# One program for the output stage and the experts of a hybrid decoder step, with the routing tables built inside the first expert block

## What is computed

```python
xp = xp + mod_p[:, 2] * yp                       # output stage
h  = modulate(x, g_ffn, shift, scale)            # RMS norm, scale and shift
top_logit, top_idx = lax.top_k(h @ w_router + b_router, 4)   # 4 of 32 experts
top_w = softmax(top_logit)
# for every expert e, in blocks of 128 of its rows:
gate = min(xb @ w_gate[e] + b_gate[e], 7)
up   = clip(xb @ w_up[e] + b_up[e], -7, 7)
f[rows] += top_w * (((up + 1) * gate * sigmoid(1.702 * gate)) @ w_down[e] + b_down[e])
y = rmsnorm(x + mod[:, 5] * f, g_final)
```

## Time and profile before

| | us |
|---|---|
| median of three timed runs | 1798.55 |
| profiled execution, its own time | 1795.53 |
| span of the profiled execution, first to last instruction | 1793.5 |
| TensorE busy in the span | 1688.0 (94%) |
| VectorE busy | 1425.5 (79%) |
| ScalarE busy | 1099.8 (61%) |

### The profile page before, as it was taken

One profiled execution on the slowest core, in us unless ns is written; L12 is line 12 of the kernel. 1 busy time (PEld: TensorE's weight loads), 2 busy tenths in 40 slices (PEclk: granted clock), 3 DMA queues, 4 the chain that ended last, 5 costly groups with the idle time before them and its releaser, 6 DMA issues.

```text
span 1793.5 us, 27031 instructions
## 1 busy us (share of the span) xinstructions
PE 1688.0 (94%) x9028; PEld 1312.8 (73%) x9028; DVE 1425.5 (79%) x1361; ACT 1099.8 (61%) x1045; POOL 333.4 (19%) x309
## 2 busy tenths in 40 slices
PE   4999978888998799999999999999999999999996
PEld 2776767555554478888888888888888888888884
DVE  4422564476426789999999999999999999999997
ACT  4212343455333367777777777777777777777773
POOL 0000021300101012223222222322222232223211
PEclk9999989699999689999999999999999999999998
DMA  9454553620226579999999999999999999999993
GB/s 348 172 185 171 107 156 101 209 96 7 77 87 200 219 269 355 382 371 377 375 378 376 371 377 376 373 375 375 378 371 381 377 373 376 382 374 374 386 351 125
DMA packets 114598, 516.08 MB, mean 288 GB/s; under 512 B 25870, under 2 KB 47710, under 8 KB 62058
## 3 DMA queue, kind: packets, MB, share of 16 engines
q1 hardware_dynamic: 101082, 483.48, 71.5%
q0 software_dynamic: 12800, 29.45, 5.9%
q10 hardware_dynamic: 656, 2.36, 0.3%
HBM read 502.75 MB, written 31.09 MB: 298 GB/s over the span
## 4 chain that ended last, share of the span: by engine, by line
PE 62%; DVE 1%; DMA 1%; ACT 0%; issue 0%; SPq 0%; POOL 0%; DVEq 0%; POOLq 0%; ACTq 0%
PE banks L2965 58%; PE banks L2973 3%; PE banks L2951 1%; DMA routing<-in_g_final 0%; DMA ffn_rows<-weighed,block_rows 0%; DVE split L3167 0%; DVE arena L3264 0%; PE banks L3020 0%; ACT split L3079 0%; DVE arena L3257 0%; DVE arena L3256 0%; SPq L2885 0%; POOL wait_taken L2903 0%; DVEq L2831 0%; DVE gates L3180 0%
## 5 line engine op out<-in xcount | busy, mean ns | idle before, releaser
L2965 PE MATMUL banks<-split 128*128 128x512 f32 x4608 | 1076.0, 393 | 1.1 <-DVE split L3167 1.1
L2965 PEld LDWEIGHTS banks<-split 128*128 128x128 f32 x4608 | 860.4, 188 | 185.9 <-issue 7.2
L3167 DVE TENSOR_TENSOR split<-expert_buffers,split 128x2048 fp32r<-128x2048 f32 x384 | 864.8, 2284 | 41.7 <-ACT split L3079 39.5
L3079 ACT ACTIVATE split<-expert_buffers 128x2048 fp32r<-128x2048 f32 x384 | 733.2, 1918 | 216.6 <-PE banks L2965 212.2
L2903 POOL TENSOR_TENSOR wait_taken<-routing 128x1 f32<-128x1 f32 x62 | 76.4, 1232 | 811.8 <-PE banks L2973 464.5
L2926 POOL DMA_INDIRECT ffn_rows<-weighed,block_rows x31 | 107.7, 3473 | 4.8 <-issue 4.8
L662 PE MATMUL banks<-w_in_high,hT_high 128*128 128x476 f32 x192 | 75.8, 395 | 4.6 <-DVE hT_low L498 4.6
L3171 DVE TENSOR_TENSOR split<-banks,split 128x1024 fp32r<-128x1024 f32 x64 | 77.8, 1215 | 0.7 <-ACT split L3082 0.7
L662 PE MATMUL banks<-w_in_high,hT_low 128*128 128x476 f32 x192 | 73.3, 382 | 0.0
L3082 ACT ACTIVATE split<-banks 128x1024 fp32r<-128x1024 f32 x64 | 64.5, 1008 | 6.1 <-PE banks L2973 6.1
L573 DVE COPY arena<-banks 128x476 f32<-128x476 f32 x12 | 7.8, 654 | 70.0 <-PE banks L662 69.9
(11 more groups left out here) (396 smaller groups left out, 1733.2 us busy)
## 6 DMA issues: line engine op xcount, KB each, us to landing
expert_buffers<-in_w_gate SPq DMA_DIRECT2D x128, 1024.0 KB, 7.8
expert_buffers<-in_w_up SPq DMA_DIRECT2D x128, 1024.0 KB, 17.9
expert_buffers<-in_w_down SPq DMA_DIRECT2D x128, 1024.0 KB, 7.4
arena<-in_w_ada SPq DMA_DIRECT2D x16, 1024.0 KB, 4.9
w_in_landing<-in_w_in SPq DMA_DIRECT2D x5, 1904.0 KB, 8.9
arena<-in_w_ada SPq DMA_DIRECT2D x4, 2048.0 KB, 19.8
arena<-in_x_prompt SPq DMA_DIRECT2D x8, 512.0 KB, 9.4
arena<-in_cache_cmp SPq DMA_DIRECT2D x32, 128.0 KB, 2.9
```

What stands on the lines that cost most here:

```text
L2965: last = pe.matmul(ps[:, bank + c, :], x[:, kt * P:(kt + 1) * P].bitcast(F32R), wt.bitcast(F32R), start=(m == 2 and kt == 0 and x is xs[0] ...
L3079: act.activation(high[:, j % RING_Q].bitcast(F32R), v, ACT.Copy).then_inc(s_high, 1)
L3167: dve.tensor_tensor(rest[:, j % RING_Q].bitcast(F32R), v, high[:, j % RING_Q], ALU.subtract).then_inc(s_rest, 1)
```

## The change

The two stages become one, `output_and_experts`, with one set of engine programs. `router_programs` returns the router's programs, of which each expert program first runs its engine's, and some late pieces as functions that are called within the first expert block.

- The first block always is expert 0. Its rows are no longer gathered: `first_rows(t)` multiplies the rows h2 of tile t (as the stationary operand, float32) with 0/1 marks `in_first`, and gives the turned block directly. `take_rank` forms these marks with two more operations.
- `take_rank(t)` and `place(t)` stand one tile earlier; `choose(3)` stands behind the rows of the last tile, not before. Tiles 3 and 4 are placed together, behind rest 2 of the first block; their shares stand behind rest 1.
- The marks and the table's sums use the rounded format, with the weight as two parts (96 columns instead of 64); the 20 matmuls of the table (`tables`) stand inside the first gate, `turn_shares` behind it, and `begin_sums` between the quarters of the first up.
- ScalarE's four first `begin_read` stand between its high parts of the first block and of block 1's gate, the fifth in step 1.
- `count_blocks` and `place_overflow` stand at the start of VectorE's step 16 (COUNT_AT), the matmuls of the marks behind TensorE's 16th up in the rounded format with 3 x 18 columns instead of 2 x 17 in float32, the second `write_table` between `read_up` and `activate` of that step, and the 16th `down` waits for it. The registers are loaded behind step 16. Until then block k is expert k, and SP loads no register for it.
- SP starts the first three weight quarters after the last output projection, the other three after the last tile's rows; the bias of expert 0 is loaded after them.

The core of the diff (in the new text; lines that were only moved are left out):

```diff
-STAGES = [project, gla, compress, prompt_attention, sample_attention, output_and_router, experts]
+STAGES = [project, gla, compress, prompt_attention, sample_attention, output_and_experts]
+COUNT_AT = 16
+WIDE = OVER + 1
...
+        def first_rows(t):
+            n = TILES[t][1]
+            pe.wait_ge(s_in_first, t + 1)
+            v = h2[t].rearrange("s (p k) -> s k p", k=KT)
+            for kt in range(KT):
+                last = pe.matmul(ps[:, 6 + kt // 4, (kt % 4) * P:(kt % 4 + 1) * P], v[0:n, kt, :], in_first[t][0:n, :],
+                                 start=(t == 0 and kt % 4 == 0), stop=(t == ST and kt % 4 == 3))
...
+        for t in range(NT):
+            project_out(t, range(KT // 2))
+            if t >= 2:
+                ranks(t - 2)
+            project_out(t, range(KT // 2, KT))
...
+            if t >= 1:
+                turn_rows(t - 1)
                 if t >= 2:
+                    first_rows(t - 2)
+                route(t - 1)
+        turn_rows(ST)
+        ranks(ST - 1)
+        route(ST)
+        first_rows(ST - 1)
+        ranks(ST)
+        first_rows(ST)
+        ranks(NT)
...
+            one = first1[0:m, t:t + 1]
+            link(dve.scalar_tensor_tensor(one, ps[0:m, 3, t * NE:t * NE + 1], 1.0, selb[0:m, t, 0:1], ALU.add, ALU.mult))
+            dve.tensor_scalar(in_first[t][0:m, :], core.const("iota_p")[0:m, :], 1.0, one, ALU.add, ALU.is_equal
...
-            gate(0, 0)
-            up(0, 4)
-            turn_rows(1, first=True)
-            overflow()
+            def first_block():
+                pe.wait_ge(s_ones, 1)
+                pe.wait_ge(router.s_lg, NT)
+                pe.wait_ge(router.s_cnt, 1)
+                start_with_bias(0, 1, GB)
+                start_with_bias(1, 1, UB)
+                pe.wait_ge(s_xt, 1)
+                product(0, (xh, xl), GB, 0, range(2))
+                pe.wait_ge(s_xt, 2)
+                product(0, (xh, xl), GB, 0, range(2, 3))
+                tables()
+                product(0, (xh, xl), GB, 0, range(3, 4))
+                turn_shares(range(ST))
+                turn_shares(range(ST, NT))
+                product(1, (xh, xl), UB, 4, range(1))
+                begin_sums(0)
+                product(1, (xh, xl), UB, 4, range(1, 2))
+                begin_sums(1)
+                product(1, (xh, xl), UB, 4, range(2, 3))
+                begin_sums(2)
+                turn_rows(1, first=True)
+                product(1, (xh, xl), UB, 4, range(3, 4))
+                begin_sums(3)
...
+                up(k, first_of(prev) + 4)
+                if counted:
+                    pe.wait_ge(s_y, prev)
+                    overflow()
                 if not last:
                     turn_rows(k + 1)
-                down(k, prev, first_of(prev) + 8, last)
+                down(k, prev, first_of(prev) + 8, last, counted)
...
# ScalarE, the first block
             high_part(0, None)
+            router_rows_T(ST)
+            weights(ST - 1)
+            high_part(1, None)
+            weights(ST)
+            first_rows_T(0)
+            for j in range(2, 7):
                 high_part(j, None)
+            shares_T()
             sigmoid(0)
             high_part(7, None)
+            begin_read(0)
+            high_part(0, 0)
+            begin_read(1)
+            high_part(1, 0)
+            begin_read(2)
+            high_part(2, 0)
+            first_rows_T(1)
+            begin_read(3)
+            high_part(3, 0)
...
# VectorE, the first block and the step
             rest_part(0, None)
+            take_rank(ST)
+            take_counts()
+            first_rest_T(0)
+            dve.wait_ge(router.s_bo, 16)
+            rest_part(1, None)
+            last_shares()
+            rest_part(2, None)
+            last_places()
+            rest_part(3, None)
+            table()
+            for j in range(4, 6):
                 rest_part(j, None)
+            shares_low()
             read_gate(0, 4)
+            for j in range(6, 8):
+                rest_part(j, None)
             rest_part(0, 0)
+            rest_part(1, 0)
+            first_rest_T(1)
             read_up(0, 8)
             activate(0)
...
+                if count:
+                    count_blocks(core, dve, linker(dve, s_dve, dve_count)).then_inc(s_counted, 1)
+                    place_overflow(core, dve, linker(dve, s_dve, dve_count)).then_inc(s_over, 1)
                 for j in range(4, 7):
                     rest_part(j, prev)
...
                 read_up(k, at + 8)
+                if count:
+                    dve.wait_ge(s_ob, 1)
+                    write_table(core, dve, linker(dve, s_dve, dve_count), NE, NSLOT, DB, WIDE).then_inc(s_tab, 1)
                 activate(k)
```

More of the change, by code:

```diff
@@ L2932, in _, with step @@
             add_rows(1, 0)
-            pool.wait_ge(s_tab, 1)
-            with pool.Fori(4, nb) as k:
+            def step(k):
                 gather(k)
@@ L2945, in _ @@
         def _(pe):
+            turn_shares, tables, begin_sums = router.tensor(pe)
             def start_with_bias(m, n, bank):
@@ L2974, in turn, with gate @@
                 last.then_inc(sem, 1)
-            def gate(k, before):
-                pe.wait_ge(s_xt, k + 1)
-                if not is_zero(k):
-                    pe.wait_ge(s_g, k)
-                    pe.wait_ge(s_u, k)
+            def gate(k, before, split=False):
+                pe.wait_ge(s_xt, 3 if split else k + 3)
+                pe.wait_ge(s_g, k)
+                pe.wait_ge(s_u, k)
                 start_with_bias(0, k + 1, GB)
                 start_with_bias(1, k + 1, UB)
-                product(0, (xh, xl), GB, before)
+                if split:
+                    product(0, (xh, xl), GB, before, range(2))
+                    pe.wait_ge(s_xt, 4)
+                product(0, (xh, xl), GB, before, range(2 if split else 0, 4))
             def up(k, before):
@@ L3107, in weigh @@
                 act.wait_ge(s_rowo, 2 * n)
-                if not is_zero(done):
+                if is_zero(done):
+                    act.wait_ge(s_begun[2], 32)
+                else:
                     act.wait_ge(s_yo, 16 * done)
@@ L3130, in step @@
                 sigmoid(k)
+                if is_zero(prev):
+                    begin_read(4)
+                    for i in range(2):
+                        act.wait_ge(s_begun[i], 32 - 16 * i)
                 acts_T(k)
@@ L3162, in _ @@
             dve.memset(ones, 1.0).then_inc(s_ones, 1)
+            take_rank, last_shares, last_places, take_counts, shares_low, table = router.vector(dve)
             def rest_part(j, prev):
@@ L3236, in _ @@
             step(1, 0)
-            with dve.Fori(2, nb1) as k:
+            with dve.Fori(2, COUNT_AT) as k:
+                step(k, k - 1)
+            step(COUNT_AT, COUNT_AT - 1, count=True)
+            dve.wait_ge(s_counted, 1)
+            nb, nb1, nb2, _ = used_blocks(dve)
+            with dve.Fori(COUNT_AT + 1, nb1) as k:
                 step(k, k - 1)
```

1004 lines of the change are left out of this document (526 added, 478 removed).

## The result

The changed kernel takes 1802.24 us (median of 20 runs, 1797.59 to 1813.38), the kernel before, measured beside it, 1797.74 (20 runs, 1793.17 to 1805.77). The ratio is 1.0026, with a 95% interval of 1.0015 to 1.0037: slower by 4.5 us, where the forecast put it. That is within the 0.3% that were called no change, but the interval leaves 1 out, so a small slowdown is shown. The profiled execution took 1807.66 us, its span is 1806.0, so it is a late one of its kind: 12.5 us longer than the span before. That difference splits exactly at points that both traces have: the router stage begins 4.4 us later (544.51 against 540.15; the stages ahead of it are unchanged), the up of step 1 comes 3.9 us earlier after that, the steps from there to block 16 take the same, block 16 takes 11.0 more and what follows it 1.0 more.

The account below looks back on a forecast made before the run. TensorE bounds the steady block (35.09 of 35.09 us), VectorE has 1.3 us to spare. Early gain -9.0 and step 16 with registers +12.6 give +3.6 on 1795.53, 1799.1; the profiled run lies 3.0 under the median, so 1802, range 1793 to 1811.

Parts of the forecast that it names:

- Last rows at 603.5: Router: first pair's rank and place fall into VectorE's transfer wait; last tile's rows come at 603.5 instead of 601.85.
- From the last rows to the first product, 14.5 us: End of router: a chain through turn, ranks, rest 0 and tile 4's matmuls; first product at 618 instead of 633.4.
- Block 0: First block: VectorE's work until 639.5, then ScalarE last; TensorE's gate of step 1 waits until 655.7.
- The gain at the up of step 1, 9.0 with 4 to 14: Before the steady blocks: the up of step 1 starts at 668.7 against 677.67, a gain of 9.0, ends 14 and 4.
- Step 16, +11.6: Step 16: VectorE's count and marks delay the 16th up about 5 us, then `down` waits for the table; loss 11.6 us.
- Register loads, 1.0: Behind step 16: TensorE loads four registers, costing from 0 to 2.8 us, taken as 1.0.
- The last part, nothing: From the last block on: only a wait on a transfer long done is added, costing nothing.
- The faster one: First block and step 16: ScalarE's reads find gaps, or `first_rows` holds the clock; -6 us, 1792.5, chance 0.14.
- The slower one: Before gate 1 and in step 16: clock falls after idle time, registers not hidden; +9, 1807.5, chance 0.31.
- The third: First block: small pieces and turns keep TensorE's clock low throughout; +24, 1822, chance 0.07.
- The low end of the range, 1793: Whole kernel: the early gain's good end, 14, with step 16 at 12.

Follow-up runs that it names:

- the version with pieces and the early read: Changed kernel with count and marks in ten pieces over VectorE's steps 6 to 15, first up read before block 1's rests: 1792.04 us, ratio 0.9969.
- the heap taken away: Changed kernel with step 16's block count written as constants, marks, their sums and second table left out: 1789.88 us, ratio 0.9964 to the kernel before.

## Why the prediction was right, point by point

- **Last rows at 603.5, 63.4 us after the stage's start: right for four profiles of ten, missed in this one (67.8).** The step that failed is that rank and place of the first tile fall into VectorE's wait for the modulation. That wait was at the last tile in the kernel before; in six profiles it stands at the first tile, where nothing fills it, and TensorE's clock falls behind it. The forecast also had `first_rows` fill only a part of TensorE's waits; it filled all of them, so this lateness goes through to the last rows. In the kernel before, eight matmuls at 560.67 took 8.81 us instead of 7.11, and a wait of 2.61 us was still left before the last rows. Why the transfer is in time in some executions stays open; that it does not decide alone is shown by the two kernels in which ScalarE issues it: there VectorE doesn't wait for it, and the rows are turned after 68.1 and 65.8 us. Nor does a fall of the clock alone: in the version with pieces and the early read the same eight records took 5.38 us, and the rows were turned after 63.4.
- **From the last rows to the first product, 14.5 us: measured 14.5.** `first_rows` was taken at 0.46 a matmul and took 0.50 to 0.52; the reason given, half clock, was wrong, for 0.50 is also its time at full clock.
- **Block 0: right.** First product to `read_gate` 19.7 us against 20.3, from there to gate 1 17.5 against 17.4, and ScalarE last, as said. Gate 1 to the up of step 1 took 13.9 against 13.0, since the fall of the clock, taken at 0.4, cost 1.6 in the gate (12.78 against 11.2), as it did before.
- **The gain at the up of step 1, 9.0 with 4 to 14: 3.9 in this profile, 9.8 with the heap taken away, 3.5 and 4.5 in two more** with the same code up to there. By the medians the change without the heap is worth 7.9, by the ratios 6.5, the 1.0 that the last part loses already taken off. The size was a little high; the profiles reach to the low end of the range and, at 3.5, just under it.
- **Step 16, +11.6: measured +11.0, right with its mechanism.** Before the up 4.61 us of waiting (5 forecast), `down` held until 34.7 us after the gate (35.2), the table last. The sums of the marks cost nothing there, but 2.42 once their cover was gone, within the 1.1 to 4.5 given.
- **Register loads, 1.0: nothing.** They lie at 1234.0 to 1236.2, under the running `down`, and no wait stands before gate 17. With this the step 16 of the forecast, 12.6, measured 11.0.
- **The last part, nothing: 1.0.** This was missed: from gate 17 to the end it is 567.5 us against 566.6. The timeline of TensorE shows, at 1781.88, a wait of 1.25 us for `ffn_rows` that the trace of before doesn't have, but that is not the cause: the two kernels without marks in step 16 don't have this wait, and take 567.7. On the chain that ended last, 0.7 us of it lie behind VectorE's last operation (4.64 us to the end of the span instead of 3.94; 4.64 and 4.67 in those two kernels as well), 0.2 in the transfer before the final norm (8.29 instead of 8.09). What lengthens them stays open.
- **The rivals.** The faster one: ScalarE's reads found no gaps, and `first_rows` didn't hold the clock. The slower one: both falls of the clock came, behind the 3.97 us before gate 1 and the 4.61 before the 16th up. The second stretched the up to 13.53 us and still cost nothing, as `down` waited for the table anyway. That and the free registers are 3.6 of the 5.5 us between 1802 and 1807.5. In two other profiles with the same step 16 a further fall, behind the table's wait, did cost 1.6 and 2.8 us. One premise of this rival was read wrongly: at 664 TensorE had not been idle, so not each fall follows a wait. The third: the clock fell for one quarter behind the table's sums (0.50 from 642 to 644) and was at 1.00 from 650 to 663 in spite of the eight turns and the bias sums there, so the small pieces did not hold it down. The Trainium skill, "TensorE: Matmul & The Clock Gate", Part 4, has it that transposes don't count as busy. No run here tests that: quarters stood between the turns, and the fall at 664 that the prediction saw as agreeing came 4.8 us after the last turn, behind 40 records of other matmuls.

The mechanism was right: an early gain that the work in step 16 more than eats up. That the sum came out within 0.3 us of 1802 is luck. Its terms were off by more, in both directions: the early gain was 9.0 and measured 3.5 to 9.8, step 16 with the registers was 12.6 and measured 11.0, the last part was nothing and measured 1.0. The low end of the range, 1793, does not follow from the terms given for it either: -14 and +12 on 1798.5 give 1796.5.

## What to carry to other kernels

Where a steady step leaves an engine 1.3 us of slack, work that is put on it should come in pieces under that: here the same operations cost 11.0 us in one step and about 3 in ten, most of it the sums on TensorE. Ask of every moved step what it cost at its old place; the marks cost about 2 us where they were. Matmuls that lie in another engine's shadow are free only until the shadow is full: after that, every slow stretch of TensorE shows. And when a wait on a transfer is used as cover, look at which consumer of the new order meets that transfer first.

## What the runs showed of the hardware

- A float32 matmul of 128 x 128 by 128 columns took 0.50 us with a stationary operand read at a stride of eight values, and 0.24 in line, at full clock. With the stride, eight took nearly the same at half clock, 4.16 us at 616 against 3.98 at 592, while in line they went from 1.95 to 3.78. Stretches of TensorE of the changed kernel at either clock (us, busy of PE, PEld, DVE, ACT, POOL, granted clock, DMA share, GB/s):

```profile
616.30:620.20 3.90, 3.90 (x17) 3.87 (x17) 3.61 (x9) 1.50 (x3) 0.00 (x0) 0.50 1.01 418
...
592.80:596.60 3.80, 3.80 (x19) 3.80 (x18) 3.70 (x5) 1.02 (x1) 0.00 (x0) 1.00 0.00 0
```

  The load of the stationary operand (the second busy time) fills the stretch in both, as it does in line. What tells the two forms apart is how long one load lasts: with the stride 336 ns at full clock and 338 at half (616 to 620); in line 192 ns at full clock and 333 at half (602 to 606). So the load with the stride didn't follow the clock, and in line it did.
- A rounded (fp32r) matmul of 128 x 128 took 0.12 us with 54 and with 96 columns alike (2.42 and 2.46 us for 20), where the float32 form with 34 columns took 0.225. The Trainium skill, "FP8 and Floating Point Precision", section "TensorE Precision Notes", gives true FP32 four passes; by that, as an estimate, a quarter of 4.50 would be 1.1 us, and the trace has 2.42. In the trace the 20 float32 matmuls are 40 records with a load of the stationary operand each, the 20 rounded ones 20, and a load lasts 192 ns in both: a record takes 0.11 to 0.12 us either way, so at this width the time goes by the number of loads. With 512 columns the trace agrees with the four passes: 0.92 us for a float32 matmul (3.68 for four), 0.23 for a rounded one (11.14 for 48).
- All profiles have a wait of 1.18 us on TensorE before the first tile's logits. With the heap taken away the granted clock stays at 1.00 behind it; in the version with pieces and the early read, with the same code up to there and no longer wait before it, it falls to 0.50, and the next eight records take 5.38 us instead of 3.68. The first product of the kernels with this router and the strided `first_rows` came 76.4 to 82.7 us after the stage's start. One profile of such a stage can't be compared with another; medians can.
